# Winograd's form for the SwiGLU up products: seven block products of half width in place of eight, with two of each weight's four sums made by accumulating DMAs

## The reference

```python
def swiglu(h, w1, w3, w2):
    return (jax.nn.silu(h @ w1) * (h @ w3)) @ w2
...
    for l in range(DEPTH_2):
        h = rmsnorm(x, g_ffn1[l])
        x = x + 0.5 * swiglu(h, w1_a[l], w3_a[l], w2_a[l])
...
        h = rmsnorm(x, g_ffn2[l])
        x = x + 0.5 * swiglu(h, w1_b[l], w3_b[l], w2_b[l])
```

## Time and profile before

| what | value |
|---|---|
| time, median of 3 | 3089.13 us (3088.85 to 3089.14) |
| profiled execution | 3089.77 us, span 3087.9 us |
| TensorE matmuls | busy 96%, 12832 |
| TensorE weight loads | busy 77%, 12832 |
| VectorE | busy 55%, 1909 |
| ScalarE | busy 41%, 1531 |
| GpSimd | busy 13%, 328 |
| DMA | 446.41 MB, mean 145 GB/s |
| granted TensorE clock, mean | 0.981 |

### The profile page before, as it was taken

One profiled execution on the slowest core, in us unless ns is written; L12 is line 12 of the kernel. 1 busy time (PEld: TensorE's weight loads), 2 busy tenths in 40 slices (PEclk: granted clock), 3 DMA queues, 4 the chain that ended last, 5 costly groups with the idle time before them and its releaser, 6 DMA issues.

```text
span 3087.9 us, 32343 instructions
## 1 busy us (share of the span) xinstructions
PE 2961.9 (96%) x12832; PEld 2370.8 (77%) x12832; DVE 1701.5 (55%) x1909; ACT 1270.0 (41%) x1531; POOL 400.2 (13%) x328
## 2 busy tenths in 40 slices
PE   8995999999959999999999999999999999999997
PEld 6674777777747888888888888888888878888886
DVE  6627888888875443366555443344434565544433
ACT  6723777777753332223233332233322333332221
POOL 3214000011002110010111110111100111111101
PEclk9996999999989999999999999999999999999999
DMA  5152999999952223222232223322232232322231
GB/s 201 59 188 92 339 352 351 351 352 353 351 191 75 96 96 93 92 92 94 95 98 96 96 96 94 97 96 96 94 95 89 89 99 94 102 92 97 95 96 58
DMA packets 126204, 446.41 MB, mean 145 GB/s; under 512 B 16096, under 2 KB 16608, under 8 KB 125792
## 3 DMA queue, kind: packets, MB, share of 16 engines
q1 hardware_dynamic: 118656, 422.37, 40.3%
q10 hardware_dynamic: 2208, 11.43, 0.9%
q0 software_dynamic: 5184, 10.50, 0.9%
HBM read 440.03 MB, written 12.58 MB: 147 GB/s over the span
## 4 chain that ended last, share of the span: by engine, by line
PE 83%; DVE 8%; issue 4%; ACT 3%; POOL 2%; DMA 1%; SPq 0%; DVEq 0%; ACTq 0%; POOLq 0%
PE bank L443 28%; PE bank L445 27%; PE bank L444 27%; DVE w_lo L1306 3%; ACT w_hi L766 2%; ACT xeT_hi L867 0%; DVE ye L1568 0%; DMA raw<-in_rec_in 0%; POOL mv L1130 0%; DVE hT_lo L1558 0%; DVE st L1376 0%; POOL w_lo L1095 0%; PE bank L449 0%; PE bank L629 0%; DVE zc L1767 0%
## 5 line engine op out<-in xcount | busy, mean ns | idle before, releaser
L1306 DVE TENSOR_TENSOR w_lo<-raw,w_hi 128x1024 fp32r<-128x1024 f32 (+3 forms) x538 | 670.8, 1255 | 473.1 <-ACT w_hi L766 470.4
L443 PE MATMUL bank<-xg_hi,w_lo 128*128 128x512 f32 x2112 | 836.5, 396 | 8.4 <-DVE xg_lo L1649 5.3
L445 PE MATMUL bank<-xg_hi,w_hi 128*128 128x512 f32 x2112 | 827.9, 392 | 0.0
L444 PE MATMUL bank<-xg_lo,w_hi 128*128 128x512 f32 x2112 | 826.6, 391 | 0.0
L766 ACT ACTIVATE w_hi<-raw 128x1024 fp32r<-128x1024 f32 (+3 forms) x548 | 561.9, 1031 | 486.6 <-PE bank L445 482.5
L443 PEld LDWEIGHTS bank<-xg_hi,w_lo 128*128 128x128 f32 x2112 | 397.8, 188 | 98.5 <-DVE xg_lo L1649 9.1
L445 PEld LDWEIGHTS bank<-xg_hi,w_hi 128*128 128x128 f32 x2112 | 397.5, 188 | 91.6
L444 PEld LDWEIGHTS bank<-xg_lo,w_hi 128*128 128x128 f32 x2112 | 397.8, 188 | 87.2 <-issue 1.7
L443 PE MATMUL bank<-g_hi,w_lo 128*128 128x512 f32 x928 | 365.1, 393 | 0.4 <-DVE g_lo L1674 0.4
L445 PE MATMUL bank<-g_hi,w_hi 128*128 128x512 f32 x928 | 363.1, 391 | 0.0
L444 PE MATMUL bank<-g_lo,w_hi 128*128 128x512 f32 x928 | 361.8, 390 | 0.0
(11 more groups left out here) (248 smaller groups left out, 2802.2 us busy)
## 6 DMA issues: line engine op xcount, KB each, us to landing
raw_more<-in_moe SPq DMA_DIRECT2D x264, 512.0 KB, 6.1
raw<-in_moe SPq DMA_DIRECT2D x120, 512.0 KB, 6.1
raw<-in_w_a SPq DMA_DIRECT2D x120, 512.0 KB, 3.3
raw<-in_w_b SPq DMA_DIRECT2D x120, 512.0 KB, 3.3
raw<-in_w_in SPq DMA_DIRECT2D x88, 512.0 KB, 3.3
raw<-in_rec_in SPq DMA_DIRECT2D x20, 512.0 KB, 4.1
raw<-in_w_o SPq DMA_DIRECT2D x16, 512.0 KB, 3.3
raw<-in_w_a SPq DMA_DIRECT2D x16, 384.0 KB, 3.1
```

Source lines behind the costliest of these rows:

```text
L443: e.matmul(out, a_lo, b_hi, start=start, stop=False)
L444: e.matmul(out, a_hi, b_lo, start=False, stop=False)
L445: return e.matmul(out, a_hi, b_hi, start=False, stop=stop)
L1306: e.tensor_tensor(lo, raw_of(k), hi.bitcast(F32), ALU.subtract).then_inc(s["lo"], 1)
```

## The change

The up products h @ w1 and h @ w3 are computed by Winograd's scheme for 2 x 2 block matrices. The hidden tiles are taken in pairs, j and j + 11 (`UP` = 11 pairs for each SwiGLU, n counts them over all four), the input tiles in pairs k and k + 4, and the tokens in halves of 256 columns (`HALF`). For each pair and each of the two matrices (m = 0 for w1, 1 for w3) there are seven products of a 128x512 weight block with one of seven forms of the input (`xf_hi`, `xf_lo`, 256 columns each), where eight products of that size would do the same plainly.

- **Input forms.** In `finish` ahead of a SwiGLU VectorE makes four half sums of each pair of input tiles in `ft`; ScalarE and VectorE split the seven forms.
- **Weight sums.** For each pair and m, four combinations of 128x512 are needed. The blocks are AB (the lower tile, as loaded), S (in `sums`) and D (a raw buffer), and E in the second half of AB's raw buffer. GpSimd's queue copies a part of w[j+11] into `sums`, adds another to it by an accumulating DMA, and adds one by an accumulating DMA into D's raw buffer; these are its six DMAs for each pair. VectorE makes the other two sums (`weight_sums`, part 0 and 1).
- **Products.** `up_pair` computes for m = 0 and 1 in turn X, Y, then adds S's product to X, computes Z, adds D's to X, E's to Z, and D's second half to X. X is kept in one bank while it grows; ScalarE copies it away between the steps (`take` into `snap`), and VectorE subtracts the copies (`first_corner`, `last_corner`, `up_first`), which gives the four quarters of the result. Signals c11, c12, c21 and c22 tell that a quarter has been read.
- **Elementwise.** `up_first` and `up_second` scale the quarters by `rsq` and multiply them after silu, now on VectorE (GpSimd's multiplications are gone).
- **Down products.** They are cut into chunks of four hidden tiles. From pair 2 to pair 9 two w2 blocks follow each pair (`down_part`: 4 results of 12 matmuls in banks 6, 7, 6, 7), each added to `xT` by a residual of its own (`down`); the last part is `down_last`.
- **Rings.** `LOOK` = 3, `NSPLIT` = 4; 9 instead of 11 raw buffers more for the experts, and one (`raw_late`) more for the layers. Signals and buffers get other names and places, and the input and output tiles are taken in the order k, k + 4.

The diff, cut to its core:

```diff
-LOOK = 2
-NRAW, NMORE, NSPLIT = 5, 11, 3
+LOOK = 3
+NRAW, NMORE, NLATE, NSPLIT = 5, 9, 1, 4
...
+            for j in range(UP):
+                for m, w in enumerate(("w1", "w3")):
+                    low, high = io[f"{w}_{name}"][l, j], io[f"{w}_{name}"][l, j + UP]
+                    fetch(("up", i, j, m, 0), (0, low, W))
+                    fetch(("up", i, j, m, 1), (0, low[:, 0:T], T), (T, high[:, T:W], T))
+                for kind in ("AB", "S", "D"):
+                    for m in range(2):
+                        block((kind, i, j, m))
+                if 2 <= j < 2 * CHUNKS:
+                    for q in range(2 * (j % 2), 2 * (j % 2) + 2):
+                        c = j // 2 - 1
+                        put(("w2", i, c, q), (0, io[f"w2_{name}"][l, 4 * c + q], W))
+            for c, q in ((CHUNKS - 1, 0), (CHUNKS - 1, 1), (CHUNKS, 0), (CHUNKS - 1, 2), (CHUNKS - 1, 3), (CHUNKS, 1)):
...
+def x_banks(n):
+    return ((0, 1), (4, 5))[n % 2]
...
+                    use(("X", n, m), "c21", 2 * n + 1 + m, x_banks(n)[m])
+                for m in range(2):
+                    use(("Y", n, m), "c11", 2 * n + 1 + m, x_banks(n + 1)[m])
+                if j == 0:
+                    use(("stat", 3 * l + 2 * (i % 2)), "rs1", 3 * l + 2 * (i % 2) + 1, 7)
+                for m in range(2):
+                    use(("Z", n, m), "c12", 2 * n + 1 + m, 2 + m)
+                if 2 <= j < 2 * CHUNKS:
+                    for pos in range(4 * (j % 2), 4 * (j % 2) + 4):
+                        use(("dn2", i, j // 2 - 1, pos), "res", res_count(i, 8 * (j // 2 - 1) + pos), 6 + pos % 2)
...
+            def terms(b, hi, lo, form, ks, start, stop):
+                x = slice(form * HALF, (form + 1) * HALF)
+                for k in ks:
+                    f = mm3(b[:, 0:HALF], hi[:, k * P:(k + 1) * P], lo[:, k * P:(k + 1) * P],
+                            xf_hi[:, k, x], xf_lo[:, k, x], start and k == ks[0], stop and k == ks[-1], True)
+                return f
...
+                else:
+                    for m in range(2):
+                        hi, lo = weights(("AB", i, j, m))
+                        xs[m] = free_bank(("X", n, m))
+                        terms(xs[m], hi, lo, 0, ks, True, True).then_inc(s["pr"], 1)
+                    for m in range(2):
+                        hi, lo = weights(("AB", i, j, m))
+                        b = free_bank(("Y", n, m))
+                        terms(b, hi[:, T:W], lo[:, T:W], 1, ks, True, True).then_inc(s["pr"], 1)
+                for m in range(2):
+                    hi, lo = weights(("S", i, j, m))
+                    e.wait_ge(s["snap"], 6 * n + 1 + m)
+                    terms(xs[m], hi[:, T:W], lo[:, T:W], 4, ks, False, True).then_inc(s["pr"], 1)
+                for m in range(2):
+                    hi, lo = weights(("S", i, j, m))
+                    b = free_bank(("Z", n, m))
+                    terms(b, hi, lo, 3, ks, True, True).then_inc(s["pr"], 1)
+                for m in range(2):
+                    hi, lo = weights(("D", i, j, m))
+                    e.wait_ge(s["snap"], 6 * n + 3 + m)
+                    terms(xs[m], hi, lo, 5, ks, False, True).then_inc(s["pr"], 1)
+                for m in range(2):
+                    e.wait_ge(s["elo"], 2 * n + 1 + m)
+                    e.wait_ge(s["snap"], 6 * n + 5 + m)
+                    terms(bank_of(("Z", n, m)), e_hi[:, m, :], e_lo[:, m, :], 2, ks, False, True).then_inc(s["pr"], 1)
+                for m in range(2):
+                    hi, lo = weights(("D", i, j, m))
+                    e.wait_ge(s["c22"], 2 * n + 1 + m)
+                    terms(xs[m], hi[:, T:W], lo[:, T:W], 6, ks, False, True).then_inc(s["pr"], 1)
...
+            def down_part(i, c, q):
+                hi, lo = weights(("w2", i, c, q))
+                if q == 0:
+                    e.wait_ge(s["glo"], GLO_FF[i] + 4 * c + 4)
+                for h in range(2):
+                    b = free_bank(("dn2", i, c, 2 * q + h))
+                    down_terms(b, hi, lo, h * T, 4 * (c % 2), 4, True, True).then_inc(s["used"] if h else s["wt"], 1)
...
+            def weight_sums(i, j):
+                n = UP * i + j
+                high = [io[f"{w}_{'ab'[i % 2]}"][i // 2, j + UP] for w in ("w1", "w3")]
+                for m in range(2):
+                    if n >= 1:
+                        k = at["S", (n - 1) // UP, (n - 1) % UP, m]
+                        e.wait_ge(*lo_signal(k))
+                        e.wait_ge(s["wsum"], 4 * (n - 1) + 3 + m)
+                    e.dma_start(sums[:, m, 0:T], high[m][:, 0:T]).then_inc(s_sum[m], 16)
+                for m in range(2):
+                    r = load_at["up", i, j, m, 1]
+                    e.wait_ge(s_raw[slot[r]], landed[r])
+                    e.dma_start(up_raw(i, j, m, 1)[:, 0:T], high[m][:, 0:T], accum_op=ALU.add).then_inc(s_sum[2 + m], 16)
+                for m in range(2):
+                    e.wait_ge(s_sum[m], 32 * n + 16)
+                    e.dma_start(sums[:, m, 0:T], high[m][:, T:W], accum_op=ALU.add).then_inc(s_sum[m], 16)
...
+            def weight_sums(i, j, part):
+                n = UP * i + j
+                for m in range(2):
+                    ab, to = up_raw(i, j, m, 0), sums[:, m, :]
+                    if part == 0:
+                        r = load_at["up", i, j, m, 0]
+                        e.wait_ge(s_raw[slot[r]], landed[r])
+                        e.wait_ge(s_sum[m], 32 * n + 32)
+                        e.tensor_tensor(to[:, T:W], to[:, 0:T], ab[:, 0:T], ALU.add).then_inc(s["wsum"], 1)
+                    else:
+                        e.wait_ge(s["wsum"], 4 * n + 1 + m)
+                        e.wait_ge(*lo_signal(at["AB", i, j, m]))
+                        e.tensor_tensor(ab[:, T:W], to[:, T:W], ab[:, T:W], ALU.add).then_inc(s["wsum"], 1)
...
+                for j in range(UP):
+                    n = UP * i + j
+                    last = at["D", i, j, 1]
+                    low(at["S", i, j, 1])
+                    if j in (1, 2):
+                        up_first(n - 1)
+                    first_corner(n)
                     if j == 0:
                         root(p)
-                    weights(c3)
-                    if FFT * i + j >= 2:
-                        e.wait_ge(s["mm"], FFT * i + j - 1)
-                    scaled(tmp[:, r, :], c1, ("w1", i, j), "uu")
-                    scaled(tmp[:, 2 + r, :], c3, ("w3", i, j), "vv")
-                    split(j, tmp[:, 2 + r, :])
-                for j in range(DT):
-                    for q in range(3):
-                        weights(at["w2", i, j, q])
-                    residual(p + 1, j, at["w2", i, j, 2], ("w2", i, j), 0.5)
+                    low(last)
+                    if j in (1, 2):
+                        up_second(n - 1)
+                    low_e(n)
+                    if j in (1, 2):
+                        up_split(n - 1)
+                    low(last + 2)
+                    last_corner(n)
+                    if j < 2:
+                        weight_sums(i, j + 1, 0)
+                        weight_sums(i, j + 1, 1)
+                    else:
+                        low(last + 4)
+                        up_first(n)
+                        c, half = j // 2 - 1, 4 * (j % 2)
+                        if j < UP - 1:
+                            weight_sums(i, j + 1, 0)
+                            down(i, 8 * c + half)
+                            up_second(n)
+                            down(i, 8 * c + half + 1)
+                            weight_sums(i, j + 1, 1)
+                            down(i, 8 * c + half + 2)
+                            up_split(n)
```

More of the change, by code:

```diff
@@ L416, in sync_program @@
                 e.dma_start(hs[:, 2 * n:2 * n + 2, :], io["xT"][:, 2 * n:2 * n + 2, :]).then_inc(s_xt[n], 16)
-            for c in range(1, NCH):
-                load(c)
+            for k in range(1, len(loads)):
+                load(k)
             for j in range(DT):
@@ new lines, in swiglu @@
+                    high(last)
+                    high_e(n)
+                    take(n, "X", 5, 1)
+                    if j in (1, 2):
+                        up_split(n - 1)
+                    take(n, "Z", 7, 2)
+                    high(last + 2)
+                    if j >= 2:
+                        high(last + 4)
+                        up_act(n)
+                        up_split(n)
+                for n in range(DT):
+                    if n == 0:
+                        high(at["w2", i, CHUNKS - 1, 3])
+                    elif n == 2:
+                        high(at["w2", i, CHUNKS, 1])
+                    elif n >= 4:
+                        weights(at["w2", i, CHUNKS, 1] + n - 7)
+                    finish(p + 1, n, "res", res_count(i, 8 * (CHUNKS - 1) + n))
@@ L1243, in mixers @@
+            e.wait_ge(s["sum"], 4 * TT - 1)
+            weight_sums(0, 0)
+            squares(0, 1, DT)
             def mixers(l):
```

(42 more changed lines are left out.)

718 lines of the change are left out of this document (490 added, 228 removed).

## The result

The changed kernel takes 3246.57 us (median of 4, 3229.77 to 3254.34) against 3089.14 us: a ratio of 1.0502, 95% interval 1.0461 to 1.0544. It is slower, by 157 us; the forecast was 3131 us, and the time lies above the range. Medians leave out one slow run, of 6010 us, among the four of the kernel e8; nothing here explains it.

What follows compares the result with a forecast made beforehand. The prediction took TensorE, busy 96% of the span, as the bound. Its terms, -96 +38 +41 +8 +24 +11 +3 +10 +3, gave +42 us on 3089.8 us: 3131 us, with an 8-in-10 range of 3050 to 3200 us.

Steps and rivals of the forecast that it cites:

- the adding DMA's price: Adding transfers into sums: 3.5 us from issue to landing, 0 to 1 us late in steady pairs; taken as 0, kept 0 to +80 us.
- the -6: Pairs 1 and 2: adding transfers landing in 2.7 us would gain 0.8 us each, -6 us.
- TensorE's work, -96: Up products: a pair's matmuls take 19.79 us in place of 21.98, over 44 pairs -96 us.
- Steady stall, +38: Pairs 2 to 9: TensorE waits 1.2 us for bank 6 until the first residual ends, +38 us.
- Pairs 1 and 2, +41: Y waits for c21 behind late sums, 6.3 us in pair 1 and 4.0 in pair 2, +41 us over four SwiGLUs.
- D behind the reciprocal, +8: Pair 0: TensorE waits about 2 us for D, whose low halves follow the reciprocal on VectorE, +8 us.
- The clock, +24: Half clock after each of the 8 long stalls costs 3 us, +24 us; steady stalls of 1.2 us cost none.
- End of a SwiGLU, +11: down_last waits 2.8 us for pair 10's hidden tiles, +11 us.
- Input forms, +13: VectorE's extra input work ahead of a SwiGLU: +3 us for three inner boundaries, +10 us at the first.
- Experts' stage, +3: The experts' stage starts 1 MB poorer with 14 raw buffers for 16, +3 us; LOOK = 3 gains nothing.
- Rival B: Adding transfers become the bound, 256 KB taking 8.7 us, part 0 late in the pairs: 3269 us; chance 0.12.
- Rival A: Stalls don't form because VectorE has slack, so the kernel gets faster: 3069 us, or 3049 with half the c21 waits; chance 0.30.

Runs made afterwards that it cites:

- e8: The kernel before with NSPLIT = 4 and 3 raw buffers in the steady ring, LOOK = 2 kept: 3072.43 us.
- e2: The changed kernel with GpSimd's adding transfers into sums issued ahead of its waits for D's loads, those into D's raw halves behind: 3079.98 us.
- e3: The changed kernel with each pair's four adding transfers made plain copies in the same queue places, leaving out the additions: 3126.89 us.
- e11: The kernel of e10 with the adding transfers made plain copies, leaving out the DMA's additions: 3010.95 us.
- e6: The kernel of e5 with square root and reciprocal moved behind the high and low halves of D and E in pair 0: 3018.57 us.
- e5: The changed kernel with e2's edit and VectorE's part 0 of the next sums moved behind the first two residuals of a steady pair: 3038.75 us.
- e1: The kernel before with the greater loading depth alone (LOOK = 3, NSPLIT = 4, 3 raw buffers in the steady ring): 3056.37 us.
- e7: The kernel of e6 with the two c21 products put first in up_first: 3012.89 us.
- e10: The kernel of e7 again, line for line the same, as a second measurement: 3017.65 us.

## Why the prediction was wrong, by its own steps

**The step that failed** is the adding DMA's price and what it hangs on: "I take 3.5 us from issue to landing" and "at 340 GB/s 11.8 us if adding costs as copying, 14.7 if double, then 2 us of latency: 23.0 to 25.9. So 0 to 1 us late", from which the sum took nothing ("I take 0"). I added up bytes, though for pairs 1 and 2 I had walked the chain; the trace has a chain, in which each link waits for the one before: 2.3 us of SyncE's issues, D's load 7.2 us (I had 3.3), 1.4 us of GpSimd, the add 7.5 us (I had 3.5; the median of all is 6.6), part 0, residual. From SyncE's first issue (1058.32) to the residual (1077.33) that is 19.0 us. Loads starting at 9.2 us, the residual comes at 28.2, where I had 25.8: 2.4 us late in this steady pair, and the same chain stands in pairs 1 and 2. What the place in the queue cost is shown by e2: 167 us. With the place alone put right the changed kernel comes to 3080 us, and its layers (first product to end) are 30 us longer than before, where the sum had +39. The price of adding, in the place as it was, is shown by e3: 120 us. The prediction had said that if adding were free of time "nothing would be gained beyond the -6". The two figures can't be added, since either edit brings the transfer nearly in time; e11 shows that adding costs little once the place is right.

The Trainium skill (DMA: Bandwidth & Descriptors, Anatomy of one DMA) fits 2.0 us plus bytes by 436 GB/s for a plain DMA of GpSimd's queue, an estimate of 2.6 us for 256 KB by that fit. The traces have more under SyncE's loads: 4.4 us in the median for the plain one in e3, and 6.6 for the adding one in its place. The sum by 2.6 us would have been still lower.

- **TensorE's work, -96:** right. Without stalls a pair takes 30.75 us (predicted 30.8), so 2.2 us less than before.
- **Steady stall, +38:** the stall without lateness is 1.14 us (predicted 1.2), as e2 shows; in the changed kernel it was 101.3 us in all.
- **Pairs 1 and 2, +41:** 59.9 us. Pair 1 waited 5.8 us (6.3 predicted), pair 2 8.8 us (4.0): the chain of DMAs from E of pair 1, again mis-sized; e2 leaves 10.6 us of the 59.9.
- **D behind the reciprocal, +8:** 13.2 us, at c22 behind the low halves of the next AB. e6 shows the reciprocal's part in it.
- **The clock, +24:** too small. "The steady stalls of 1.2 us cost none" holds for 1.14 us, but they were 3.0 us on average and up to 5.7. Busy time fell by 41 us where the work gives -96 and the experts' stage -30 (575.7 to 545.8), so the clock took about 85 by this difference, of which e5 gives back 63.
- **End of a SwiGLU, +11:** 11.4 us, right.
- **Input forms, +13:** TensorE waits 20.3 us for xf_lo, 8.8 us once at the first input and 2.2 us for `xg_lo`, for which the kernel before had 5.3 us: +26, twice what I had.
- **Experts' stage, +3:** the sign was wrong. I said that LOOK = 3 "only changes stages that have no stall of weight to lose", from a DMA share of 93% in the middle of the stage; it gained 39 us, and e1 gives 34.5 of it to the depth. That hid a fifth of the loss: without it the result would be some 3285 us.
- **Rival B** came near in time (3269 us) with a part of its mechanism: the adds were late by 2 to 3 us, but mostly since they were issued late and close together, and DMA engines were 43% busy, not the bound. **Rival A** is what e5 and e7 are, by order and not by slack.

What stays open: why D's load takes 7.2 us where one of 512 KB took 3.3 us before. It is the second of two parts of 256 KB and the last of six loads issued together, GpSimd's DMAs run beside them, and no run separates these. The medians of SyncE's 512 KB loads are 5.8 us after and 6.1 us in e2, so the place of the adds isn't the cause.

## What to carry to other kernels

Walk a new DMA's chain link by link, with the latency of each under the traffic it will meet, and don't divide bytes by bandwidth: the DMA engines were 43% busy when this one became the bound. In an in-order queue, issue first what is ready and needed first; three lines moved there were worth 167 us, more than the 96 us of matmuls that the scheme saves. And look at what a changed constant does by itself: the buffer depth gives 34 us without any of the scheme. And two measurements of one program (e7 and e10) differ by 5 us here, so a step of that size tells nothing by itself.

## What the runs showed of the hardware that was not expected

- An adding DMA of 256 KB lands 6.6 us after issue (median of 88 in the changed kernel) where a plain one in its place needs 4.4 (e3). Issued ahead of the other adding DMAs it lands in 4.2 (e2), a plain one there in 3.2 (e11). It occupies GpSimd for 0.9 to 1.2 us in place of 0.55.
- Of the DMA engines' time it takes about twice as much per byte, as an estimate from the queue lines. The change brings 69.2 MB to GpSimd's queue, which had 0.9% of DMA time before (28 us of the span). As copies they took 7.4% of 3127 us less these 28 in e3, 204 us or 2.9 us per MB. In the changed kernel they took 11.6% of 3244 us less 28, 348 us. Two of the six DMAs of each pair stay copies (23.1 MB, 68 us at that price), so the four adding ones took 280 us for 46.1 MB, 6.1 us per MB. The queue's packets are 37568 in place of 26304, 64 more for each of the 176 adding DMAs.
- A stall of 1.14 us in each pair left the clock at 1.00 (e2). In the changed kernel, where they were 3.0 us on average, the one of 3.95 us was followed by a stretch near half clock (0.67 over 8 us).
